# Where the norm factor is applied in a two-block transformer kernel: on the operands, or on the products' results

## The reference

```python
def rms_norm(x, g):
    y = x * lax.rsqrt(jnp.mean(x * x, axis=-1, keepdims=True) + EPS)
    return y * g

# block 1
z = rms_norm(h, attn_norm) @ w_in                       # queries, keys, values, gates of two mixers
h = h + concat([sparse_attention(z), gated_linear_attention(z)]) @ w_out
u = causal_dwconv(rms_norm(h, ffn_norm) @ w_up, conv_w, conv_b)     # 3 taps along the tokens
gate, up = split(u)
h = h + (silu(gate) * up) @ w_down
# block 2, with 16 meta tokens put ahead of the 512
proj = rmsnorm(h, norm_mix_gain) @ w_in                 # 11 groups of columns, 3 of them convolved with 4 taps
h = h + merge(delta_rule(proj), stick_breaking_attention(proj), gates) @ w_out
h = h + (silu(gate(n)) * up(n)) @ w_down                # n = rmsnorm(h, norm_ffn_gain)
```

## Time and profile before

| | us |
|---|---|
| times of three runs | 2434.31, 2425.79, 2431.33 (median 2431.33) |
| the profiled execution's own time | 2439.5 |
| its span on the core | 2437.7 |
| mean granted clock of PE | 0.97 of full |
| PE, DVE, ACT busy | 2294.1, 1024.9, 840.9 |

### The profile page before, as it was taken

The page is one execution under the profiler, slowest core; times in us unless marked ns, Lnnn a source line. Parts: engine busy times, 40 slices in busy tenths (PEclk is TensorE's granted clock), DMA queues, the critical chain, the costliest instruction groups (busy, mean ns, idle before and its releaser), DMA issues. The chain is left out here.

```text
span 2437.7 us, 32841 instructions
## 1 busy us (share of the span) xinstructions
PE 2294.1 (94%) x13732; PEld 1763.6 (72%) x13732; DVE 1024.9 (42%) x1625; ACT 840.9 (34%) x1436; POOL 36.4 (1%) x68
## 2 busy tenths in 40 slices
PE   4999788999999799989998999999999999999999
PEld 4777456788888687986765788666565577888887
DVE  3355575655522455653334323334331254333322
ACT  2433453444422442332224222234245533222211
POOL 0000000000000000000000000000011100000000
PEclk9999899999999898999999999999899999999999
DMA  3224001222222142331214321124511142232222
GB/s 121 75 68 147 18 1 52 78 95 95 95 95 87 54 148 97 124 110 58 74 53 148 114 88 61 63 96 168 175 57 40 44 156 69 96 95 92 94 92 94
DMA packets 78307, 218.63 MB, mean 90 GB/s; under 512 B 8400, under 2 KB 12880, under 8 KB 78160
## 3 DMA queue, kind: packets, MB, share of 16 engines
q1 hardware_dynamic: 78160, 216.53, 26.8%
HBM read 185.69 MB, written 29.75 MB: 88 GB/s over the span
## 5 line engine op out<-in xcount | busy, mean ns | idle before, releaser
L294 PE MATMUL ps<-nx_hi,whi 128*128 128x512 f32 (+1 forms) x1968 | 735.0, 373 | 47.3 <-PEq L707 24.6
L295 PE MATMUL ps<-nx_lo,whi 128*128 128x512 f32 (+1 forms) x1968 | 702.9, 357 | 0.0
L296 PE MATMUL ps<-nx_hi,wlo 128*128 128x512 f32 (+1 forms) x1968 | 702.4, 357 | 0.0
L279 DVE TENSOR_TENSOR wlo<-raw,whi 128x1024 fp32r<-128x1024 f32 x282 | 344.6, 1222 | 532.3 <-ACT whi L272 531.7
L294 PEld LDWEIGHTS ps<-nx_hi,whi 128*128 128x128 f32 x1968 | 379.0, 193 | 138.4 <-issue 58.5
L272 ACT ACTIVATE whi<-raw 128x1024 fp32r<-128x1024 f32 x282 | 297.6, 1055 | 422.1 <-PE ps L296 347.2
L296 PEld LDWEIGHTS ps<-nx_hi,wlo 128*128 128x128 f32 x1968 | 380.0, 193 | 53.3
L295 PEld LDWEIGHTS ps<-nx_lo,whi 128*128 128x128 f32 x1968 | 381.7, 194 | 49.7 <-issue 1.9
L294 PE MATMUL ps<-act_hi,whi 128*128 128x512 f32 x352 | 139.6, 396 | 0.0
L295 PE MATMUL ps<-act_lo,whi 128*128 128x512 f32 x352 | 139.1, 395 | 0.0
L296 PE MATMUL ps<-act_hi,wlo 128*128 128x512 f32 x352 | 139.0, 395 | 0.0
(11 more groups left out here) (432 smaller groups left out, 2661.4 us busy)
## 6 DMA issues: line engine op xcount, KB each, us to landing
raw<-stream_dram SPq DMA_DIRECT2D x285, 512.0 KB, 3.5
qk_spill<-ring SPq DMA_DIRECT2D x16, 264.0 KB, 2.1
qk_cols<-qk_spill SPq DMA_DIRECT2D x16, 264.0 KB, 3.9
v_spill<-ring SPq DMA_DIRECT2D x16, 264.0 KB, 2.1
v_cols<-v_spill SPq DMA_DIRECT2D x16, 264.0 KB, 4.3
dz_spill<-ring SPq DMA_DIRECT2D x16, 256.0 KB, 2.1
dz<-dz_spill SPq DMA_DIRECT2D x16, 256.0 KB, 4.3
sbk_spill<-ring SPq DMA_DIRECT2D x8, 264.0 KB, 2.1
```

What stands on the lines that cost most here:

```text
L279: dve.tensor_tensor(K.wlo[:, n % HL], K.raw[:, n % RAW], K.whi[:, n % HL].bitcast(F32), ALU.subtract).then_inc(K.s_lo, 1)
L294: pe.matmul(out, whi, xhi, start=start, stop=False, skip_group_check=skip)
L295: pe.matmul(out, whi, xlo, start=False, stop=False, skip_group_check=skip)
L296: return pe.matmul(out, wlo, xhi, start=False, stop=stop, skip_group_check=skip)
```

## The change

The factor no longer goes onto the operands. They become h · gain, split as soon as a tile of h is complete, and the factor, made beside the products, is multiplied onto each PSUM tile as it is read. In block 1's FFN, where three readers share a PSUM tile, DVE multiplies the tile in place. `start` is gone: a new lane `Head` is woven into the first stage. At block 2's begin a lane `Factor` takes the last tile's square, the sums, the root and the spread. In `Stored`, `Convolved` and `GateProduct` the multiplication on DVE takes the place of ACT's copy; `Convolved`'s first tap goes from DVE to ACT. `Delta`'s yields move ahead of its waits, and some buffers are shared or shorter (`dt` with `x2`; the ring beside stick-breaking attention has 2 places, not 3).

```diff
+def scaled_hi(act, x, gain, hi):
+    return act.activation(hi, x, ACT.Copy, scale=gain)
+def scaled_lo(dve, x, gain, hi, lo):
+    return dve.scalar_tensor_tensor(lo, x, gain, hi.bitcast(F32), ALU.mult, ALU.subtract)
+def factor_made(K, dve, z, rs, bank=SPREAD_BANK):
+    dve.wait_ge(z["root"], 1)
+    dve.reciprocal(K.t_rs[:], K.t_rs[:]).then_inc(z["factor"], 1)
+    dve.wait_ge(z["spread"], 1)
+    dve.tensor_copy(rs, K.ps[:, bank, :]).then_inc(z["factor_made"], 1)
...
 # out_ffn, PE
-                pe.wait_ge(za["squares"], KT)
-                norm_sums(K, pe, za, KT - 1, sq[:, (KT - 1) % 2])
-                norm_spread(K, pe, za)
                 for u in range(2 * FT):
...
+                    if u == 0:
+                        factor_sums(K, pe, z, KT - 1, sq[:, (KT - 1) % 2])
+                    if u == 1:
+                        factor_spread(K, pe, z)
...
 # out_ffn, ACT, up phase of block 1
-                    act.wait_ge(K.s_used, s + 1)
...
+                    act.wait_ge(z["scaled"], 2 * p + 1 if conv else p + 1)
                     if conv:
-                        act.activation(g[:, pb], K.ps[:, (KT + 2 * p) % 4, :], ACT.Identity, scale=w1[:, 0, p:p + 1, 2],
+                        act.activation(g[:, pb], ps[0], ACT.Identity, scale=w1[:, 0, p:p + 1, 2],
                                        bias=b1[:, 0, p:p + 1]).then_inc(z["first_tap"], 1)
-                        hi_of(act, s, s, 0)
+                        if p > 0:
+                            hi_of(act, s, s, 0)
...
 # out_ffn, DVE, up phase
+                        dve.wait_ge(K.s_used, s + kind + 1)
+                        if conv or kind == 0:
+                            dve.tensor_tensor(ps, ps, rs[:], ALU.mult).then_inc(z["scaled"], 1)
+                            if conv:
+                                if p > 0 or kind == 1:
+                                    lo_of(dve, s + kind, s + kind, 0)
+                                dve.wait_ge(z["first_tap"], 2 * p + kind + 1)
...
-                        lo_of(dve, s + kind, s + kind, 0)
...
 # Convolved, DVE
+                dve.tensor_tensor(z[:, 3 + a:3 + e], K.ps[:, self.bank(c, h), 0:e - a], self.rs[:, a:e], ALU.mult).then_inc(self.free, 1)
+            split_next_lo(K, dve, self.first + c)
...
 # Head, SP and PE
+        sp.dma_start(K.param[:, a:a + n], v["param"][:, a:a + n]).then_inc(z["gain_in"], 16)
+        load_chunk(K, sp, 0)
+        for i in range(4):
+            sp.dma_start(K.h[:, 2 * i:2 * i + 2], v["x"][:, 2 * i:2 * i + 2]).then_inc(z[f"x_in_{i}"], 16)
+        load_chunk(K, sp, 1)
+        sp.dma_start(K.const[:], v["const"][:, 0:K.const.shape[1]]).then_inc(z["consts_in"], 16)
...
+        yield 0.99
+        pe.wait_ge(z["consts_in"], 16)
+        for d in range(KT):
+            factor_sums(K, pe, z, d, self.sq[:, d % 4], 0)
+        yield 1.99
+        factor_spread(K, pe, z, 1)
```

More of the change, by code:

```diff
@@ L381, in norm_scale @@
[L381 to L462, removed]
@@ L474, in out_ffn @@
     n_all = n_out + 2 * FT + FT
[L475 to L478, removed]
+    names = ("out_done", "mix_done", "added", "scaled", "first_tap", "convolved", "silu", "act_full", "act_hi", "act_lo", "x_hi", "x_lo",
+             "next_squares", "next_sums", "next_hi") + FACTOR_SEMS
+    z = dict(zip(names, sems(K, *names)))
+    zn = {"squares": z["next_squares"], "sums": z["next_sums"]}
     w1 = par(K, "conv1_w").rearrange("p (k f t) -> p k f t", k=2, t=3)
@@ L580, in _ @@
                         hi_of(act, first + d // per, first + d // per, 0)
-                    square(za, d, d + 1)
-                norm_root(K, act, za)
-                norm_hi(K, act, za, xn)
+                    act.wait_ge(z["added"], d + 1)
+                    scaled_hi(act, K.h[:, d], gain_ffn[:, d:d + 1], x_tile(d)[0]).then_inc(z["x_hi"], 1)
+                    square(z, d, d + 1)
+                factor_root(K, act, z)
                 for p in range(FT):
                     pb, s = p % 2, up0 + 2 * p
-                    act.wait_ge(K.s_used, s + 1)
+                    ps = [K.ps[:, (KT + 2 * p + kind) % 4, :] for kind in range(2)]
@@ L857, with __init__ @@
     RING = 3
-    def __init__(self, K, z_sb, ring, taps, dst, banks, z, t0, t1):
-        self.z, self.ring, self.taps, self.dst = z_sb, ring, taps, dst
-        self.conv, self.silu, self.stored = z["convolved"], z["silu"], [z[s] for s in STORED_SEMS]
+    def __init__(self, K, z_sb, ring, taps, dst, rs, banks, z, t0, t1):
+        self.z, self.ring, self.taps, self.dst, self.rs = z_sb, ring, taps, dst, rs
+        self.conv, self.silu, self.tapped, self.stored = z["convolved"], z["silu"], z["tapped"], [z[s] for s in STORED_SEMS[:3]]
         super().__init__(K, len(dst), lambda c: (K.nx_hi, K.nx_lo, FULL), banks, z, t0, t1)
@@ L909, with __init__, dve @@
 class GateProduct(Products):
-    def __init__(self, K, dst, banks, z, t0, t1):
-        self.dst = dst
+    def __init__(self, K, dst, rs, made, banks, z, t0, t1):
+        self.dst, self.rs, self.made = dst, rs, made
         super().__init__(K, 1, lambda c: (K.nx_hi, K.nx_lo, FULL), banks, z, t0, t1)
-    def evac_act(self, act, c, h, a, e, ps):
-        self.wait_piece(act, c, h)
-        act.activation(self.dst[:, a:e], ps, ACT.Copy).then_inc(self.free, 1)
+    def dve(self, dve):
+        yield self.at(1.0)
+        split_next_lo(self.K, dve, self.first)
+        yield self.at(1.0) + 0.2
+        dve.wait_ge(self.made, 1)
+        for h, (a, e) in enumerate(FULL):
+            self.wait_piece(dve, 0, h)
+            dve.tensor_tensor(self.dst[:, a:e], self.K.ps[:, self.bank(0, h), 0:e - a], self.rs[:, a:e], ALU.mult).then_inc(self.free, 1)
 GATE_SEMS = ("gate_t", "gate_x", "gate_ln", "gate_g", "gate_cum", "gate_e", "gate_made")
@@ new lines, with __init__, act, pe @@
+class Factor(Lane):
+    def __init__(self, K, rs, c, t0, z):
+        super().__init__(t0, t0)
+        self.K, self.rs, self.z, self.sq = K, rs, z, scratch(K, c, "last_sq", [P, SEQ])
+    def act(self, act):
+        yield -1.0
+        act.activation(self.sq[:], self.K.h[:, KT - 1], ACT.Square).then_inc(self.z["last_square"], 1)
+        factor_root(self.K, act, self.z)
+    def pe(self, pe):
+        K, z = self.K, self.z
+        yield self.t0
+        pe.wait_ge(z["last_square"], 1)
+        for t in range(TT):
+            mm = pe.matmul(K.ps[:, SUM_BANK, t:t + 1], self.sq[:, t * P:(t + 1) * P], cst(K, "ones")[:, 0:1],
+                           start=False, stop=True, skip_group_check=True)
+        mm.then_inc(z["sums"], 1)
+        yield self.t0 + 0.6
+        factor_spread(K, pe, z)
+    def dve(self, dve):
+        yield -1.0
+        dve.memset(self.rs[:, 0:META], 1.0)
+        factor_mean(self.K, dve, self.z, 1)
+        factor_made(self.K, dve, self.z, self.rs[:, META:T2])
@@ L1951, in __init__ @@
         self.n = sum(1 if kind == "col" else 4 for kind, _ in jobs)
         K.at += self.n
+        self.freed = []
+        cols = rows = 0
+        for kind, _ in jobs:
+            for _ in range(1 if kind == "col" else TT):
+                cols, rows = (cols + 1, rows) if kind == "col" else (cols, rows + 1)
+                self.freed.append((self.free_col, cols) if kind == "col" else (self.free_row, rows))
     def places(self):
@@ L2004, in act @@
                 yield self.at((c + 1) / self.n)
-                act.wait_ge(K.s_used, self.first + c + 1)
-                act.activation(dst, self.tile(q), ACT.Copy).then_inc(self.free, 1)
                 split_next_hi(K, act, self.first + c)
@@ L2017, in act @@
                     act.wait_ge(self.piece, p + t + 1)
-                act.activation(dst[:, t], self.tile(q + t), ACT.Copy).then_inc(self.free, 1)
+                act.activation(dst[:, t], self.tile(q + t), ACT.Copy, scale=K.t_rs[:, t:t + 1]).then_inc(self.free_row, 1)
             split_next_hi(K, act, self.first + c + 3)
     def dve(self, dve):
-        for c in range(self.n):
-            yield self.at((c + 1) / self.n)
-            split_next_lo(self.K, dve, self.first + c)
+        K = self.K
+        for kind, dst, c, q, _ in self.places():
+            for u in range(1 if kind == "col" else 4):
+                yield self.at((c + u + 1) / self.n)
+                if kind == "row" or c == 0:
+                    split_next_lo(K, dve, self.first + c + u)
+                if kind == "col":
+                    dve.wait_ge(self.made, 1)
+                    dve.wait_ge(K.s_used, self.first + c + 1)
+                    dve.tensor_tensor(dst, self.tile(q), self.rs, ALU.mult).then_inc(self.free_col, 1)
+                    if c > 0:
+                        split_next_lo(K, dve, self.first + c)
     def sp(self, sp):
```

439 lines of the change are left out of this document (287 added, 152 removed).

## The result

Four runs gave a median of **2404.22 us** (2397.14 to 2407.66), against 2432.82 for the kernel before in its four runs: a ratio of 0.9884, 95% interval 0.9852 to 0.9916, 28.6 us less. The forecast was 2402, with a range of 2380 to 2424. The profiled execution took 2407.66, its span 2405.9.

A forecast was written before the change was run, and what follows sets the result against it. TensorE (PE), busy 94% of the span, was taken as the bound. Terms -24.7 + 12.0 - 12.2 - 8.5 + 2.5 + 1.9 = -29.0 took 2439.5 us profiled to 2410.5, or 2402 as median; range 2380 to 2424.

The forecast's parts named there:

- The start: Kernel start: first product near 8.1 us, sums behind it, second product and spread done near 36.8; -24.7 us (-19.7 to -29.6).
- Rival D: Kernel start gives back about 10 us through shared memory, slow sums and a late second product; 2412 us, chance .10.
- FFN 1: Block 1's FFN: earlier first up product (-7.6 us) and a binding chain of DVE and ACT steps (+19.6), together +12.0.
- The transition: Block 1, output projection to up products: products follow directly, last sums and spread behind them; -7.6 us.
- the thread: Block 1's up products: DVE and ACT steps run as one chain, 12.29 us a pair against PE's 11.20; +19.6 us.
- rival B: Block 1's up products: the DVE and ACT chain does not bind, 11.2 us or less a pair; 2383 us, chance .20.
- Rival C: Block 1's FFN: PE's clock falls from short waits in each pair, 8.3 us more a pair; about 2568 us, chance .07.
- Block switch: Block 1's FFN to block 2: first product starts 14.4 us earlier, sums and spread return beside the gate product; -12.2 us.
- Second FFN: Before the second FFN: first tile at 2062.0 instead of 2070.58 us, PE staying the bound; -8.5 us.
- DVE's copies: Block 2's projections: PSUM copies moved from ACT to DVE mostly lie beside PE's work; +2.5 us (-1 to +12).
- rival F: Block 2: late banks, DVE costing 1 us at each of some 32 chunks, 32 more; 2434 us, no change, chance .10.
- the rest of block 2: All of block 2's projections: DVE copies +2.5 us, last convolution chunk and last gate's tanh +1.9; +4.4 together.

The follow-up runs named there:

- Both cuts of the thread: Two runs on the changed kernel, block 1's up phase: DVE splits the next chunk behind the taps, 2389.06 us; or ACT rounds it before waiting for the multiplication, 2389.81 us.
- two experiments here: Each atop the split behind the taps (2389.06 us): start's sums between the second product's matmuls, 2373.62 us; block 2's gate steps set later, 2376.16 us.

## Why the prediction was right

**The start** was forecast at -24.7 and is -25.2. The first product came at 8.69, not 8.1; the sums took 10.1 where the middle of the bounds was 10.7. The sum is right for the reason given, and one reason was only half seen: the sums are slow because the clock falls during them, and the second product pays for it too. Put between matmuls they cost 5 us less. Rival D, the start giving back 10, did not come.

**FFN 1.** The transition gave -8.0 (forecast -7.6), the thread 12.32 us a pair (12.29) and +20.7 (+19.6). Both cuts of the thread took all of that back, and one multiplication more in each half lengthened it by 1.47 to 13.79 a pair. So rival B, that the thread doesn't bind, is out, and that a thread over two engines binds, while each is idle for a third of the time or more, is shown. What let it bind was not the multiplication alone: with the split behind the taps, as before the change, the multiplication and the thread's other steps fit under PE's pace.

**Rival C**, a falling clock in FFN 1, did not come: the clock was 1.00 with .9 us of waiting in 12.3. But with 2.1 in 13.8 it did fall, six times. What the prediction cites beside C (the Trainium skill, "TensorE: Matmul & The Clock Gate", section "A second HAM failure mode: psum-queue depth-cycling") tells of a kernel in which frequent short idle pieces between groups of matmuls made the clock go up and down. The trace of the doubled multiplication agrees, that of the changed kernel doesn't. One reading beside C was off: the clock did not fall at 418 but at 421.6, behind 5.3 us in which PE had only sums and the spread to do.

```profile
420.00:421.60 1.60, 1.06 (x8) 0.87 (x8) 0.50 (x1) 0.00 (x0) 0.00 (x0) 1.00 0.64 251
421.60:428.40 6.80, 5.02 (x12) 3.70 (x13) 6.76 (x12) 3.78 (x6) 0.00 (x0) 0.50 0.02 9
```

**Block switch.** -13.0 at the first products (forecast -12.2). That place lies ahead of the spread, which the forecast counts there; behind the spread it is -12.0, so 1.0 of the +3.2 in the table's next line belongs here. The other 2.3 went at the gates' step, where I had named the gate product and the first chunk as cover and stopped there. ACT's step for the gates, 6.4 us with four table loads from 815.43 to 821.82, stands ahead of a chunk's rounding and first tap; DVE's taps wait for that, and DVE takes the gates behind them:

```profile
815.43 0.24 ACT L981 ACTIVATE e<-xa 128x40 f32<-128x40 f32 x1 [0.16 <-DVE xa L960]
...
821.58 0.24 ACT L985 ACTIVATE beta<-b_rows 128x40 f32<-128x40 f32 x1
```

The kernel before paid for this step as well: PE stood 3.15 us for a copy on ACT that came behind it.

```profile
847.77 0.39 PE L294 MATMUL ps<-nx_hi,whi 128*128 128x264 f32 x1 [3.15 <-ACT z L875]
```

With the change it is 4.21, so the stand itself grew by 1.1; the rest of the 2.3 comes from a longer stretch of low clock there (6.8 us against 3.4) and a wait of .75 a little later. Moving the step gave back 4.1, more than the change had lost there.

**Second FFN**: -8.8, forecast -8.5, PE-bound as said. **DVE's copies** (+2.5 with rival F at +32): little cost found even when doubled, so rival F is out. What I called +4.4 for the rest of block 2 came out at +2.7, but by the clock's chance and the gates, not by the steps I named. With other profiles of the same kernels it is -1.0 to +9.1: that the number was near there, and with it the total to within some 2 us, is luck; that the start, the two transitions, the thread and the block switch came out near is not.

## What to carry to other kernels

Moving a multiplication from operands to results took the chain of a norm off the path at all four places, but the engines that now read the results need room for it: without that, block 1's FFN lost 20.7 us. Add up the steps that hand over to each other between two engines, whatever the busy share of each, and compare with the period of the engine that bounds; if the sum is longer, first look for an independent step (here the split of later weights) that can stand where an engine waits. Small PE work was cheaper between large matmuls here: 5 us less for 64 one-column matmuls at the start.

## What was not expected

The clock's stretches at half speed vary between executions of one kernel at the same instruction: 3.4 and 23.9 us behind the same 4 us stand, worth 8.8 us. A difference of a few microseconds between two kernels in a stage that neither changed is not evidence, while a stage without such a stretch repeats to some tenths of a microsecond. The same goes for medians of a few runs: those of two experiments here lie 9 to 10 us further under their base than the places that were edited account for.
